# Second attention layer: cached keys turned by VectorE during the feed-forward before it, kept in DRAM and loaded turned

## What is computed

```
k_all = concatenate([cache_k, k], axis=1)      # (8, 256 + 16, 16, 64): 256 cached rows, 16 new ones
s = einsum('bqhd,bkhd->bhqk', q, k_all) / 8 + forget terms, masked
p = softmax(s);  o = einsum('bhqk,bkhd->bqhd', p, v_all);  out = o @ w_out
```

## Time and profile before

| what | value |
|---|---|
| median of 3 runs | 1882.85 us (1882.59 to 1884.51) |
| span of the profiled execution | 1885.1 us |
| TensorE busy / weight load / VectorE / ScalarE / GpSimd | 98% / 87% / 52% / 38% / 12% |
| mean granted TensorE clock | 0.997 of full speed |
| bytes moved by DMA | 259.38 MB, mean 138 GB/s |
| up half of layer 2's feed-forward | about 1098 to 1280 us of the span |
| second attention layer, its 16 steps | about 1487 to 1567 us of the span |

### The profile page before, as it was taken

One profiled execution on the slowest core, in us unless ns is written; L12 is line 12 of the kernel. 1 busy time (PEld: TensorE's weight loads), 2 busy tenths in 40 slices (PEclk: granted clock), 3 DMA queues, 4 the chain that ended last, 5 costly groups with the idle time before them and its releaser, 6 DMA issues.

```text
span 1885.1 us, 29064 instructions
## 1 busy us (share of the span) xinstructions
PE 1849.9 (98%) x12004; PEld 1642.4 (87%) x12004; DVE 983.0 (52%) x1569; ACT 722.0 (38%) x1144; POOL 225.9 (12%) x357
## 2 busy tenths in 40 slices
PE   8999999999999999999999999999999999999998
PEld 8777799998888887799998899998897777999986
DVE  4557653443567778743443664443465576543434
ACT  4246443333255454333332343333242463433321
POOL 3114070000011222230000100000031230000000
PEclk9999999999999999999999999999999999999999
DMA  7357254433353433444433434433364562444332
GB/s 246 128 203 229 81 160 123 129 129 123 117 164 105 125 116 104 118 139 125 124 134 123 146 101 125 132 124 125 110 206 150 200 221 90 137 132 124 128 129 79
DMA packets 179171, 259.38 MB, mean 138 GB/s; under 512 B 14717, under 2 KB 122349, under 8 KB 179040
## 3 DMA queue, kind: packets, MB, share of 16 engines
q1 hardware_dynamic: 161184, 197.18, 32.3%
q0 software_dynamic: 17856, 60.35, 9.9%
HBM read 243.19 MB, written 13.19 MB: 136 GB/s over the span
## 4 chain that ended last, share of the span: by engine, by line
PE 90%; DVE 4%; ACT 3%; issue 1%; DMA 1%; SPq 0%; DVEq 0%; ACTq 0%
PE ps L1605 14%; PE ps L1607 14%; PE ps L1606 14%; PE ps L1617 11%; PE ps L1615 11%; PE ps L1616 11%; PE ps L1833 1%; PE ps L1951 1%; PE ps L1938 1%; PE ps L1638 1%; PE ps L1888 1%; PE ps L1671 1%; DVE w_lo L785 1%; PE ps L1908 1%; PE ps L1673 1%
## 5 line engine op out<-in xcount | busy, mean ns | idle before, releaser
L785 DVE TENSOR_TENSOR w_lo<-w_raw,w_hi 128x1024 fp32r<-128x1024 f32 x370 | 452.1, 1228 | 709.1 <-ACT w_hi L439 707.9
L439 ACT ACTIVATE w_hi<-w_raw 128x1024 fp32r<-128x1024 f32 x370 | 389.3, 1059 | 803.5 <-DMA w_raw<-in_w_ffn_in_dram 363.1
L1605 PE MATMUL ps<-xT_hi,w_hi 128*128 128x384 f32 x1568 | 528.4, 337 | 2.5 <-issue 1.4
L1607 PE MATMUL ps<-xT_hi,w_lo 128*128 128x384 f32 x1568 | 527.0, 336 | 0.0
L1606 PE MATMUL ps<-xT_lo,w_hi 128*128 128x384 f32 x1568 | 526.9, 336 | 0.0
L1605 PEld LDWEIGHTS ps<-xT_hi,w_hi 128*128 128x128 f32 x1568 | 294.8, 188 | 5.2 <-issue 5.1
L1606 PEld LDWEIGHTS ps<-xT_lo,w_hi 128*128 128x128 f32 x1568 | 294.8, 188 | 0.1
L1607 PEld LDWEIGHTS ps<-xT_hi,w_lo 128*128 128x128 f32 x1568 | 294.8, 188 | 0.0
L1617 PE MATMUL ps<-w_hi,hT_lo 128*128 128x512 f32 x528 | 210.6, 399 | 0.0
L1616 PE MATMUL ps<-w_lo,hT_hi 128*128 128x512 f32 x528 | 208.1, 394 | 0.0
L1615 PE MATMUL ps<-w_hi,hT_hi 128*128 128x512 f32 x528 | 207.4, 393 | 0.0
(11 more groups left out here) (329 smaller groups left out, 2021.8 us busy)
## 6 DMA issues: line engine op xcount, KB each, us to landing
w_raw<-in_w_ffn_in_dram SPq DMA_DIRECT2D x352, 256.0 KB, 3.2
w_raw<-in_w_ffn_out_dram SPq DMA_DIRECT2D x176, 256.0 KB, 2.9
w_raw<-in_w_fox_in_dram SPq DMA_DIRECT2D x96, 256.0 KB, 2.9
k_c<-in_cache_fox_k_dram POOLq DMA_DIRECT2D x32, 512.0 KB, 5.3
v_c<-in_cache_fox_v_dram POOLq DMA_DIRECT2D x32, 512.0 KB, 4.0
w_raw<-in_w_hgrn_in_dram SPq DMA_DIRECT2D x64, 256.0 KB, 2.9
w_raw<-in_w_fox_out_dram SPq DMA_DIRECT2D x32, 256.0 KB, 2.9
out_dram<-kv_tok POOLq DMA_DIRECT2D x4, 1024.0 KB, 5.0
```

The costliest lines, as they stand in the source:

```text
L439: nc.scalar.activation(w_hi[:, slot, :], w_raw[:, slot, :], ACT.Copy).then_inc(hi_ready, 1)
L785: V.tensor_tensor(w_lo[:, slot, :], w_raw[:, slot, :], w_hi[:, slot, :].bitcast(F32), ALU.subtract).then_inc(lo_ready, 1)
L1605: mm(out, w_hi[:, slot, cols], x_hi[:, k, :], start=k == 0, stop=False, skip_group_check=True)
L1607: last = mm(out, w_lo[:, slot, cols], x_hi[:, k, :], start=False, stop=k == KD - 1, skip_group_check=True)
```

## The change

For layer 3 (AHEAD) alone; layer 0 stays as it is.

- GpSimd, in layer 2's feed-forward: eight loads of a stream's cached keys into one buffer `k_nat` (1 MB; partition p holds rows 2p and 2p + 1), each after the one before it was turned.
- VectorE, in chunks c = 1 to 8 behind `hT_lo`: two transposes of 128x1024 numbers in blocks of 32x32, from `k_nat` to the one buffer `k_turn`, for stream c - 1. The first waits for the load, and for the end of the store before.
- SP, in chunks c = 3 to 10 behind the four unit loads: waits for the turn of stream c - 3, then four stores from `k_turn` to a DRAM tensor `keys_t`. Each takes 32 partitions; every piece that is contiguous on both sides has 64 numbers (256 bytes), 1024 pieces to a store.
- SP, in layer 3: sixteen loads of turned keys `k_t` (128 partitions x 4 x 256 numbers, pieces of 1 KB), three ahead of unit 20, the others behind the sixth unit of the output product, each after the scores three steps before.
- GpSimd, in layer 3: no `k_c` loads; a copy of the 16 new keys into `k_t` for each step (`new_keys`).
- TensorE: no `s_keys`; the scores read `k_t` and wait for its load and for `new_keys`. ScalarE and VectorE: no copies to `ktc`.
- Placement: `k_t` lies over `k_c` and a little beyond, `v_c` starts behind it; the third `v_c` load waits for the forget sums (`c_lo`) instead of unit 12. A wait on a constant (`eps_set`) is gone.

The order of the other calls within a step is the same.

```
+        keys_t = nc.dram_tensor("keys_t", [DB, D, PAST], F32)
...
+        k_t = sb("k_t", [P, KV, 4, PAST + DT], after("rcp"))
+        v_c = sb("v_c", [P, KV, 2, WCOLS], after("k_t"))
...
+            def turned_keys(i, first, end):                       # SP
+                f = FOX[i]
+                for n in range(first, end):
+                    b, hf = n // 2, n % 2
+                    if n < KV:
+                        sync.wait_ge(*at(KEYS["stored"], 64 * DB))
+                        sync.wait_ge(unit_used, START[i]["mix"])
+                    else:
+                        sync.wait_ge(*at(f["s_scores"], n - KV + 1))
+                    sync.dma_start(k_t[:, n % KV, :, 0:PAST], keys_t[b, hf * WCOLS:(hf + 1) * WCOLS, :].rearrange(
+                        "(g p) k -> p g k", p=P)).then_inc(KEYS[f"in{n % KV}"][0], 16)
+            def store_turned(b):                                  # SP
+                sync.wait_ge(*at(KEYS["turned"], b + 1))
+                for r in range(4):
+                    sync.dma_start(keys_t[b].rearrange("(c d) k -> d c k", d=32)[:, :, 64 * r:64 * r + 64],
+                                   k_turn[32 * r:32 * r + 32, :, :, :].rearrange("d c k a -> d c (k a)")).then_inc(KEYS["stored"][0], 16)
...
+                    if i == AHEAD:
+                        chunks(w_fox_in[j], s["mix"], 6, 0, 5 * CU)
+                        turned_keys(i, 0, KV)
+                        chunks(w_fox_in[j], s["mix"], 6, 5 * CU)
+                        chunks(w_fox_out[j], s["out"], 2, 0, RING)
+                        turned_keys(i, KV, 2 * DB)
+                        chunks(w_fox_out[j], s["out"], 2, RING)
...
+                    if i + 1 == AHEAD and 3 <= c < CF:            # SP, after the four loads of chunk c
+                        store_turned(c - 3)
...
+                    if i + 1 == AHEAD and 1 <= c <= DB:           # VectorE, after hT_lo of chunk c
+                        turn_keys_ahead(c - 1)
+            def turn_keys_ahead(b):
+                dve.wait_ge(*at(KEYS["loaded"], 16 * (b + 1)))
+                if b:
+                    dve.wait_ge(*at(KEYS["stored"], 64 * b))
+                for a in range(2):
+                    ins = V.transpose(k_turn[:, :, :, a], k_nat[:, a, :])
+                ins.then_inc(KEYS["turned"][0], 1)
...
+                def new_keys(n):                                  # GpSimd
+                    now = slice(SEQ + DT * (n // 2), SEQ + DT * (n // 2) + DT)
+                    G.tensor_copy(k_t[:, n % KV, :, PAST:], kT[:, 4 * (n % 2):4 * (n % 2) + 4, now]).then_inc(KEYS["new"][0], 1)
...
+            def cached_keys(i, j):                                # GpSimd, layer 2's feed-forward
+                pool.wait_ge(unit_used, START[i - 1]["up"] + 2)
+                for b in range(DB):
+                    if b:
+                        pool.wait_ge(*at(KEYS["turned"], b))
+                    pool.dma_start(k_nat[:, :, :], cache_fox_k[j, b].rearrange("(p a) h d -> p a (h d)", a=2)).then_inc(KEYS["loaded"][0], 16)
...
                 def s_pairs(n):                                   # TensorE
                     if n:
                         pe.wait_ge(*at(f["s_exp"], n))
-                    pe.wait_ge(*at(f["kt_a"], n + 1))
-                    pe.wait_ge(*at(f["kt_d"], n + 1))
+                    if i == AHEAD:
+                        pe.wait_ge(*at(KEYS[f"in{n % KV}"], 16 * (n // KV + 1)))
+                        pe.wait_ge(*at(KEYS["new"], n + 1))
...
-                    if 2 <= n < HEADS:
+                    if 2 <= n < HEADS and i != AHEAD:
                         s_keys(n, KT_BANKS)
```

More of the change, by code:

```diff
@@ L235, in trunk_program @@
         scale_bc = sb("scale_bc", [P, D], after("hist"))
+        k_nat = sb("k_nat", [P, 2, D], after("h32"))
+        k_turn = sb("k_turn", [P, D // 32, 32, 2], after("k_nat"))
         assert after("sq") <= after("h32")
@@ L303, in trunk_program @@
         y_stored = sem("y_stored")
+        H = HGR[KINDS.index("hgrn")]
+        KEYS = {"loaded": (H["st0_in"][0], 16 * (HG // 2)), "stored": (x_in[0], 16),
+                "turned": (H["snew"][0], 2 * HG), "new": (H["gate"][0], 2 * GRP),
+                "in0": (x_in[1], 16), "in1": (x_in[2], 16), "in2": (turned_in, 0)}
         CT_AFTER, CT_BANK, CT_LF = (8, 9, 10, 11, 12), (7, 3, 7, 3, 7), 4
@@ L380, in _ @@
                 if kind == "fox":
-                    chunks(w_fox_in[j], s["mix"], 6, 0 if i else 1)
-                    chunks(w_fox_out[j], s["out"], 2)
+                    if i == AHEAD:
[5 more added lines that the diff above has]
+                        chunks(w_fox_out[j], s["out"], 2, RING)
+                    else:
+                        chunks(w_fox_in[j], s["mix"], 6, 1)
+                        chunks(w_fox_out[j], s["out"], 2)
                 elif kind == "hgrn":
@@ L547, in fox @@
                 for u in range(6 * CU):
-                    if u == 6 * CU - 2:
+                    if u == 6 * CU - 2 and i != AHEAD:
                         act.wait_ge(*at(f["ktr"], 1))
@@ L1035, in fox @@
                                         negate=True).then_inc(f["nmax"][0], 1)
-                        if n:
+                        if n and i != AHEAD:
                             key_sides(n, KT_BANKS + 1)
@@ L1338, in fox @@
                 assert laid == LAID
-                pool.wait_ge(unit_used, m0 + 12)
-                load_k(KV - 1)
+                if i == AHEAD:
+                    pool.wait_ge(*at(f["c_lo"], 3))
+                else:
+                    pool.wait_ge(unit_used, m0 + 12)
+                    load_k(KV - 1)
                 load_v(KV - 1)
                 pool.wait_ge(*at(f["laid"], LAID))
+                def new_keys(n):
+                    now = slice(SEQ + DT * (n // 2), SEQ + DT * (n // 2) + DT)
+                    G.tensor_copy(k_t[:, n % KV, :, PAST:], kT[:, 4 * (n % 2):4 * (n % 2) + 4, now]).then_inc(KEYS["new"][0], 1)
                 def store(n, marked, kp, ks):
@@ L1361, in fox @@
                 pool.wait_ge(*at(f["kT_a"], KD))
+                if i == AHEAD:
+                    for n in range(KV):
+                        new_keys(n)
                 pool.wait_ge(*at(f["kstored"], 16 * 2))
@@ L1371, in fox @@
                 for n in range(KV, 2 * DB + KV):
-                    if n < 2 * DB:
+                    if n < 2 * DB and i == AHEAD:
+                        pool.wait_ge(*at(f["s_scores"], n - KV + 1))
+                        new_keys(n)
+                    elif n < 2 * DB:
                         pool.wait_ge(*at(f["ktr"], n - KV + 1))
@@ L1933, in s_pairs @@
                         pe.wait_ge(*at(f["s_exp"], n))
-                    pe.wait_ge(*at(f["kt_a"], n + 1))
-                    pe.wait_ge(*at(f["kt_d"], n + 1))
+                    if i == AHEAD:
+                        pe.wait_ge(*at(KEYS[f"in{n % KV}"], 16 * (n // KV + 1)))
+                        pe.wait_ge(*at(KEYS["new"], n + 1))
+                    else:
+                        pe.wait_ge(*at(f["kt_a"], n + 1))
+                        pe.wait_ge(*at(f["kt_d"], n + 1))
                     for g in range(4):
                         rows, k = slice(32 * g, 32 * g + 32), 4 * (n % 2) + g
-                        mm(ps[rows, SS_BANK, 0:PAST + DT], qs[:, k, n // 2, :, :].rearrange("p e q -> p (e q)"), ktc[:, g, :],
+                        keys = k_t[:, n % KV, g, :] if i == AHEAD else ktc[:, g, :]
+                        mm(ps[rows, SS_BANK, 0:PAST + DT], qs[:, k, n // 2, :, :].rearrange("p e q -> p (e q)"), keys,
                            start=True, stop=False, skip_group_check=True)
@@ L1972, in fox @@
                         pe.wait_ge(*at(f["v_d"], 1))
-                    if n == 1:
+                    if n == 1 and i != AHEAD:
                         s_keys(n, KT_BANKS)
```

30 lines of the change are left out of this document (18 added, 12 removed).

## The result

The changed kernel takes 1919.45 us (median of 4 runs, 1917.91 to 1922.66) against 1883.68 us (1882.59 to 1886.96) of the kernel before on the same chip: a ratio of 1.0191, with a 95% interval of 1.0177 to 1.0205. The forecast was 1889.3 us with a range from 1873 to 1916. The sign was right, the size wrong by 30 us.

A forecast was written before the change was run, and what follows sets the result against it. TensorE, busy 98% of the span, was taken to bound the kernel. 8.6 us gained in attention and 15 us lost in layer 2's feed-forward gave +6.5 us, 1889.3 us from a median of 1882.85, range 1873 to 1916 us.

The forecast's parts named there:

- The loop through SP's queue: Layer 2's feed-forward: SP's stores delay weight loads, hence the next SiLU and transposes; each of eight chunks slips 3.1 us.
- stand: TensorE's waiting in layer 2's feed-forward: eight slips, 24.6 us, less 9.5 us of slack, 15 us, from chunk 7.
- L: Time from `turned` to the landing of the load gating the next SiLU: taken as 12.2 us; at most 9.1 closes the loop.
- The issues: L counted by SP's issues: four stores 6.7 us, two units' issues 1.2 and 0.6, landing 3.2; 11.7 us.
- the engines: L counted by DMA work: stores 5.7 us, `k_nat` 2.8, two units 3.4, landing remainder 2.35; at most 14.3 us.
- The issue durations: SP's store issues grow by 1.44 ns per further piece: 1.68 us for 1024 pieces, 6.7 us for four stores.
- The gain: Layer 3's attention: TensorE loses its key turns, 0.55 us in each of 14 steps plus 0.87 us; 8.6 us in sum.
- the edit at nothing: Layer 3's later third `v_c` load, needed some 25 us after `c_lo`, was claimed hidden, at no cost.
- The loop closes: Rival in layer 2's feed-forward: L at most 10.3 us, gain whole, 1874.2 us; loop closed or nearly had chance 0.33.
- Heavy pieces: Rival: 256-byte stores cost a read and write, 11.5 us per four, L about 18, stand 62 us, 1936 us; chance 0.1.
- Gain smaller: Rival in layer 3's attention: scaled probabilities or `pT_s` bind harder, gain 3 us, 1895 us with the stand; no separate chance.
- `k_t` loads and `new_keys`: Layer 3: loads issued three steps, over 12 us, ahead against 5.3 us to land, and the key copy, both hidden, no cost.

The follow-up runs named there:

- first experiment: Changed kernel with each stream's four stores moved behind the chunk's second unit load, one chunk later: 1880.62 us, ratio 0.9980 to the kernel before.
- big pieces: Changed kernel with each store moving its 256 KB in 256 pieces of 1 KB, not 1024 of 256 bytes: 1903.97 us, ratio 1.0097 to the kernel before.
- wait alone: Changed kernel with stores on GpSimd's queue; SP keeps its wait for `turned` at the old place, no store behind it: 1896.87 us, ratio 1.0058.
- both: Changed kernel with stores in 1 KB pieces and `k_nat` loaded for stream 0 alone: 1886.96 us, ratio 1.0008 to the kernel before.

## Why the prediction came out as it did

- **The loop through SP's queue** was right in place, mechanism and count. The way from the gating `w_hi` over `hT_lo` to the end of the transposes takes 7.33 us (predicted 7.51), eight chunks slip, TensorE waits for `h`, if from chunk 5 on and not from chunk 7, since each slip was twice as large. Order alone (first experiment) removes the whole stand.
- **The step that failed** is the choice of L: "The issues give 11.7, the engines up to 14.3; I take 12.2, near the issues, since the 2.35 us and the averaged 53 ns hold waits that a full queue doesn't add." Measured 15.25 us, in the prediction's own terms 7.5 us for the stores' issue (6.7), 3.0 us for the issue of the two units (1.8) and 4.6 us for the landing (3.2). But issue durations do not set L by themselves (big pieces: 5.3 us less issue, 2.1 us less L), and even a queue of their own for the stores leaves 13.9 us. The sum of the DMA engines' work was the nearer term, and it was still 1 us short. Its parts were close: 2.1 us for small pieces against 1 KB ones (predicted 5.7 - 3.4 = 2.3), 2.0 us for `k_nat` (predicted 2.8). It left out what stands behind the gating load: in the 15.25 us 3.35 MB were moved (3.8 MB in L of "big pieces", 3.95 MB in "wait alone"), where stores, `k_nat` and two units are 3.1 MB; how much of the missing us that is, no run shows. At 8 us of time for 1 us of L, 15.25 - 12.2 = 3.05 us is 24.4 us of the miss of 30. By the engines' sum of 14.3 the forecast would have been 8 (14.3 - 12.2) = 17 us higher, 1906 us.
- **The issue durations** were predicted at 1.7 us each, 6.7 for four; four take 7.5 to 8.3 us, in the last chunk 4.0. That this nearly fits is no support: on GpSimd's queue the same stores issue in 0.79 us each, and on SP's with a quarter of the pieces and the same bytes the four take 2.25 us.
- **The gain** was predicted as 8.6 us and is 6.6. The step's part was right (0.51 against 0.55 us per step, `pT_s` late by 0.34 us). Wrong was the edit at nothing: "the later third `v_c` load" was costed by its own data, needed late, and not by what is queued behind it on GpSimd, the output of 1.5 MB, which came out in front of a weight load on the path. With that order mended and the new values first, the stage gives 8.3 us.
- **The rest of the miss**, 30.2 us less 24.4: 2.0 us of gain that did not come, 1.1 us of stand beyond the 39.4 that L gives from the forecast's 15 (the lower clock behind the last wait, 1.6 us, is a price that the prediction did not have), 0.8 us by which the kernel before lies higher in these runs, and some 2 us that the marks, which are of one execution of each kernel, do not show.
- **The rivals.** *The loop closes*: not here; 11.4 us as the break-even of L was right, as "both" shows, with L at 11.5 and a ratio of 1.0008. *Heavy pieces*: no. A piece of 256 bytes cost more per byte than one of 1 KB, but that is 2.1 us of 15.25, not a doubling of the store. The Trainium skill (DMA: Bandwidth & Descriptors, Specifications) asks for 512 bytes or more because below it the engine reads, modifies and writes; these runs show a surcharge of about 2 us for the 4096 pieces of a stream, and not the 11.5 us of that case. *Gain smaller*: by 2 us, for another reason than the one named.
- **`k_t` loads and `new_keys`** cost nothing, as said: no wait of TensorE for either.

## What to carry to other kernels

When an edit puts a wait into a DMA queue that also carries the main stream, follow the chain from what is waited for, through the queue and the DMA engines, to the next thing that is waited for; if it returns to itself within a period, its excess over the period is paid in every turn. Time from such a wait to a landing by the bytes that all queues start at that moment (here 3.3 to 4.0 MB in 13 to 15 us, parts of the units behind the gating one among them), not by the issue durations. And cost a moved wait by what is queued behind it: here a load needed late held back 1.5 MB that then ran into a load on the path. A wait of TensorE can cost more than its length: behind one of 2.2 us the lower clock took another 3.3 us.

## What the runs showed of the hardware

- The issue of one and the same store (32 partitions, 1024 pieces of 256 bytes) takes from 0.31 to 5.88 us on SP's queue and 0.78 to 0.82 us on GpSimd's. On SP's, four in the same chunk take 7.5 us, and 4.0 us when the 1 MB load of `k_nat` is not under way:

```profile
L402 SPq DMA_DIRECT2D keys_t<-k_turn x32: 308/826/5877, 1139.0 to 1302.0; - x32
```

- Two queues share the DMA engines such that loads on one are not ahead of 2 MB issued at about the same time on the other: 13.9 us to the landing of the second unit, where 15.25 us is what it takes behind the stores on the same queue. From 1165 to 1172 us of "wait alone" 414 packets of GpSimd's queue brought 1.80 MB, 465 of SP's 0.45 MB.
- The granted clock of TensorE went to its lower level (0.50, 1.2 GHz) behind all waits for `h` of 2.7 to 6.0 us in these kernels, and stayed there for 2.9 to 6.1 us. Shorter waits differ: behind 1.94, 1.96, 2.21, 2.22 and 2.34 us it fell, behind 1.85, 1.99, 2.11, 2.22 and 2.41 us it stayed at 1.00. In none of the kernels without the stand did TensorE wait for `h`.
- VectorE's transpose of 128x1024 float32 in blocks of 32x32, written with stride two, takes 1.20 to 1.25 us, the same as an elementwise operation with as many numbers per partition (1.23 us).
